# Splitting each weight piece of the down product in one instruction instead of two

## What is computed

```python
D_MODEL = 1024; SEQ = 512; DEC_BATCH = 8; DEC_SEQ = 8; D_FF = 4 * D_MODEL

def decoder_layer(x, shift0, s0, kv_past, logf_past, lw):
    ...
    x = x + mix @ lw['w_out']
    h2 = rms_norm(x, lw['mlp_norm'])
    x = x + jnp.square(jax.nn.relu(h2 @ lw['w_mlp_up'])) @ lw['w_mlp_down']
```

## Time and profile before

| | |
|---|---|
| median of 3 executions | 933.12 us (929.53 to 935.15) |
| the profiled execution, its own time | 931.69 us |
| its span, first to last instruction | 930.0 us |
| TensorE busy | 893.5 us (96%) |
| VectorE busy | 640.7 us (69%) |
| ScalarE busy | 451.7 us (49%) |
| mean granted TensorE clock, share of full speed | 0.996 |

### The profile page before, as it was taken

One profiled execution on the slowest core, in us unless ns is written; L12 is line 12 of the kernel. 1 busy time (PEld: TensorE's weight loads), 2 busy tenths in 40 slices (PEclk: granted clock), 3 DMA queues, 4 the chain that ended last, 5 costly groups with the idle time before them and its releaser, 6 DMA issues.

```text
span 930.0 us, 21268 instructions
## 1 busy us (share of the span) xinstructions
PE 893.5 (96%) x8588; PEld 768.9 (83%) x8588; DVE 640.7 (69%) x1083; ACT 451.7 (49%) x771; POOL 62.0 (7%) x95
## 2 busy tenths in 40 slices
PE   6999999999899999899999999999999999999998
PEld 5999899998887767666655789988998899889986
DVE  5563377647656773666564572789988988988796
ACT  6422536313241376685562543463575456535751
POOL 0000112114500000000000000100101000000000
PEclk9999999999999999999999999999999999999999
DMA  8542787762200677548897704896878722443343
GB/s 271 181 137 69 160 204 202 238 128 68 83 6 3 216 264 245 199 158 298 308 391 263 250 15 137 209 273 185 246 204 239 214 91 93 179 136 92 133 142 144
DMA packets 73163, 164.47 MB, mean 177 GB/s; under 512 B 5918, under 2 KB 32126, under 8 KB 70890
## 3 DMA queue, kind: packets, MB, share of 16 engines
q1 hardware_dynamic: 59370, 124.26, 38.9%
q0 software_dynamic: 13696, 38.85, 17.6%
HBM read 156.55 MB, written 40.10 MB: 211 GB/s over the span
## 4 chain that ended last, share of the span: by engine, by line
PE 81%; DVE 13%; ACT 2%; issue 2%; DMA 1%; DVEq 0%; ACTq 0%
PE PS L960 16%; PE PS L962 15%; PE PS L961 15%; PE PS L1152 7%; PE PS L1315 3%; PE PS L1387 2%; PE PS L1337 2%; PE PS L993 2%; DVE WL L2912 2%; PE PS L1301 2%; PE PS L1423 1%; PE PS L1275 1%; PE PS L1292 1%; PE PS L1627 1%; PE PS L1628 1%
## 5 line engine op out<-in xcount | busy, mean ns | idle before, releaser
L961 PE MATMUL PS<-WL,U 128*128 128x512 f32 x224 | 87.5, 391 | 0.0
L960 PE MATMUL PS<-WH,U 128*128 128x512 f32 x224 | 87.5, 390 | 0.0
L2025 ACT ACTIVATE WH<-Wraw 128x1024 fp32r<-128x1024 f32 x56 | 57.9, 1055 | 47.8 <-DMA Wraw<-tau 16.3
L2912 DVE TENSOR_TENSOR WL<-Wraw,WH 128x1024 fp32r<-128x1024 f32 x56 | 66.8, 1218 | 7.1 <-ACT WH L2025 7.1
L1152 PE MATMUL PS<-AR 64*64 64x64 f32 x1912 | 61.8, 219 | 4.6 <-issue 2.9
L1152 PEld LDWEIGHTS PS<-AR 64*64 64x64 f32 x1912 | 58.6, 135 | 8.1 <-issue 5.8
L960 PE MATMUL PS<-WR,HR 128*128 128x384 f32 (+1 forms) x184 | 63.7, 346 | 0.8 <-issue 0.8
L960 PE MATMUL PS<-h2H,WH 128*128 128x288 f32 x208 | 61.4, 295 | 0.5 <-DVE rc L3034 0.5
L961 PE MATMUL PS<-h2L,WH 128*128 128x288 f32 x208 | 61.2, 294 | 0.0
L962 PE MATMUL PS<-h2H,WL 128*128 128x288 f32 x208 | 61.2, 294 | 0.0
L1315 PE MATMUL PS<-cst,AR 128*128 128x128 f32 x384 | 53.5, 281 | 7.0 <-ACT W L1913 7.0
(11 more groups left out here) (436 smaller groups left out, 2309.2 us busy)
## 6 DMA issues: line engine op xcount, KB each, us to landing
AR<-in_cache_kv SPq DMA_DIRECT2D x120, 384.0 KB, 4.7
tau<-in_w_mlp_down POOLq DMA_DIRECT2D x24, 1024.0 KB, 9.1
Wraw<-tau SPq DMA_DIRECT2D x16, 1024.0 KB, 4.8
Wraw<-in_w_mlp_up SPq DMA_DIRECT2D x14, 1024.0 KB, 5.6
Wraw<-in_w_mlp_down SPq DMA_DIRECT2D x12, 1024.0 KB, 5.1
W<-in_w_in SPq DMA_DIRECT2D x6, 1536.0 KB, 8.9
QK<-in_cache_kv SPq DMA_DIRECT2D x8, 384.0 KB, 5.9
AR<-in_x_prompt SPq DMA_DIRECT2D x4, 512.0 KB, 7.0
```

Source lines behind the costliest of these rows:

```text
L960: mm(out, lH, rH, start=start, stop=False, skip_group_check=skip)
L961: mm(out, lH, rL, start=False, stop=False, skip_group_check=skip)
L2025: f(piece_half(WH, r, d, h), piece_half(Wraw, r, d, h), ACT.Copy).then_inc(w_hi, 1)
L2912: tt(piece_half(WL, r, d, h), piece_half(Wraw, r, d, h), piece_half(WH, r, d, h).bitcast(F32), SUB).then_inc(w_lo, 1)
```

## The change

Each piece of the down product is split by one ScalarE instruction and one VectorE instruction of 2048 columns, in place of two of each of 1024. `w_hi` and `w_lo` then grow by one a piece. TensorE's use of a piece is still counted by halves. The order of the instructions moves where the halves stood apart:

```diff
-        def split_at(r, d, h):
-            return 4 + 14 * r + 2 * d + h + 1
+        def split_at(r, d):
+            return 4 + 7 * r + d + 1
...
-        def half_free(r, d, h):
+        def piece_free(r, d):
 
             if d >= 2:
-                return dn_used, 14 * r + 2 * (d - 2) + h + 1
-            return pair_used(4 * r - 1, 2 * d + h) if r else (u_ps, 6 + 2 * d)
+                return dn_used, 14 * r + 2 * (d - 2) + 2
+            return pair_used(4 * r - 1, 2 * d + 1) if r else (u_ps, 6 + 2 * d)
...
-                    def split(h):
-
-                        pe.wait_ge(w_hi, split_at(r, d, h))
-                        pe.wait_ge(w_lo, split_at(r, d, h))
-
+                    pe.wait_ge(w_hi, split_at(r, d))
+                    pe.wait_ge(w_lo, split_at(r, d))
...
-            def half_hi(r, d, h):
+            def down_hi(r, d):
 
                 q = 11 * r + 4 + d
-                act.wait_ge(*half_free(r, d, h))
+                act.wait_ge(*piece_free(r, d))
                 act.wait_ge(in_raw[q % 2], 16 * (q // 2))
-                f(piece_half(WH, r, d, h), piece_half(Wraw, r, d, h), ACT.Copy).then_inc(w_hi, 1)
+                f(whole_piece(WH, r, d), whole_piece(Wraw, r, d), ACT.Copy).then_inc(w_hi, 1)
...
-                half_hi(r, 1, 0)
+                down_hi(r, 1)
                 relu_crossed(i)
                 square_quad(i, 1)
                 square_quad(i, 0)
-                half_hi(r, 1, 1)
                 mix_form_hi(r, 2)
                 down_splits(r)
...
-                half_lo(r, 2, 0)
-                half_done(r, 0)
+                piece_done(r, 0)
                 take_common(r, X_BANK, ADD if r else None)
-                half_lo(r, 2, 1)
+                down_lo(r, 2)
...
-                half_lo(r, 6, 0)
-                half_done(r, 4)
+                down_lo(r, 6)
+                piece_done(r, 4)
                 take_quarter(0, 1, Q5_BANK, ADD)
                 take_samples(1, S_BANKS[1], ADD)
-                half_lo(r, 6, 1)
...
                 crossed_sums(i)
-                half_lo(r, 1, 0)
+                down_lo(r, 1)
                 quad_low(i)
-                half_lo(r, 1, 1)
                 take_down(r)
```

More of the change, by code:

```diff
@@ L564, in piece_half, with whole_piece @@
             return ring[:, s, h * 1024:(h + 1) * 1024].rearrange("p (k c) -> p k c", k=2)
-        def half_free(r, d, h):
+        def whole_piece(ring, r, d):
+            return ring[:, (11 * r + 4 + d) % 2 if ring is Wraw else (d + r) % 2, :]
+        def piece_free(r, d):
             if d >= 2:
-                return dn_used, 14 * r + 2 * (d - 2) + h + 1
-            return pair_used(4 * r - 1, 2 * d + h) if r else (u_ps, 6 + 2 * d)
+                return dn_used, 14 * r + 2 * (d - 2) + 2
+            return pair_used(4 * r - 1, 2 * d + 1) if r else (u_ps, 6 + 2 * d)
         def pair_used(i, p):
@@ L2127, in down_splits @@
                         turned_hi(4)
-                    for h in range(2):
-                        half_hi(r, d, h)
+                    down_hi(r, d)
             def turned_hi(n):
@@ L2147, in _ @@
                 if n in (5, 7):
-                    for h in range(2):
-                        half_hi(0, n // 2 - 2, h)
+                    down_hi(0, n // 2 - 2)
                 if 4 <= n < 7:
@@ L2907, in sample_low, with down_lo @@
                 tt(HL[:, row, NS:2 * NS], us_raw[:, m % 2, :], HL[:, row, 0:NS].bitcast(F32), SUB).then_inc(u_lo, 1)
-            def half_lo(r, d, h):
-                dve.wait_ge(w_hi, split_at(r, d, h))
-                tt(piece_half(WL, r, d, h), piece_half(Wraw, r, d, h), piece_half(WH, r, d, h).bitcast(F32), SUB).then_inc(w_lo, 1)
+            def down_lo(r, d):
+                dve.wait_ge(w_hi, split_at(r, d))
+                tt(whole_piece(WL, r, d), whole_piece(Wraw, r, d), whole_piece(WH, r, d).bitcast(F32), SUB).then_inc(w_lo, 1)
             def mix_form_lo(r, d):
@@ L3061, in take_down @@
                 mix_sum(r, 4)
-                half_done(r, 1)
+                piece_done(r, 1)
                 take_quarter(1, 1, Q7_BANK, SUB)
-                half_lo(r, 3, 0)
-                half_lo(r, 3, 1)
+                down_lo(r, 3)
                 mix_form_lo(r, 4)
-                half_done(r, 2)
+                piece_done(r, 2)
                 take_quarter(0, 0, X_BANK, ADD)
                 take_samples(0, S_BANKS[0], ADD)
-                half_lo(r, 4, 0)
-                half_lo(r, 4, 1)
+                down_lo(r, 4)
                 mix_form_lo(r, 5)
-                half_done(r, 3)
+                piece_done(r, 3)
                 dve.wait_ge(y_ready, 10 * r + 3)
                 take_quarter(1, 1, Q5_BANK, ADD)
-                half_lo(r, 5, 0)
-                half_lo(r, 5, 1)
+                down_lo(r, 5)
                 mix_form_lo(r, 6)
@@ L3088, in take_down @@
                     form_lo(4 * r, 0)
[L3089 removed]
+                piece_done(r, 5)
                 take_common(r, X_BANK, SUB)
@@ L3112, in _ @@
                 if n in (5, 7):
-                    for h in range(2):
-                        half_lo(0, n // 2 - 2, h)
+                    down_lo(0, n // 2 - 2)
                 if 4 <= n < 7:
```

15 lines of the change are left out of this document (5 added, 10 removed).

## The result

Seven executions of each kernel on one chip: before 932.98 us in the median (929.53 to 935.71), after **942.19 us** (939.39 to 946.25). The ratio is 1.0091, with an interval of 1.0068 to 1.0115 (95%): 8.5 us slower. The prediction said 7.4 us more, 940.5 (936.5 to 944.0).

A forecast was written before the change was run, and what follows sets the result against it. The prediction took TensorE, busy 893.5 of 930.0 us, as the bound, so only later operands count. Its terms, 3.4 + 2.4 + 1.0 + 0.6 = 7.4 us, on the median of 933.12 gave 940.5 us, range 936.5 to 944.0.

The forecast's parts named there:

- The saving: All 28 pieces: wholes save 2.0 us of VectorE and 2.5 us of ScalarE time; worth nothing where TensorE does not wait.
- Round 0, 3.4 us: Lateness of TensorE at the end of round 0, from later whole splits: 3.4 us, ends 2.5 and 4.2.
- Piece 1: Round 0, piece 1: first product in steady flow at 616.7 in place of 614.30, TensorE 2.4 us late.
- The wait at `take_samples`: Round 0, at 623.43, where VectorE's chain sets the time: TensorE no longer idles 0.76 us; lateness there 1.6 us.
- piece 3: Round 0, piece 3: no slack, VectorE's whole starts 1.5 us later and TensorE's lateness becomes 2.5 us.
- Ends of rounds 1 and 2: Taking of piece 5 comes 3.0 us later against 2.0 us of slack: TensorE waits 1.2 us each, 2.4 us together.
- End of round 3: VectorE starts taking piece 5 at 921.23 in place of 920.21, and all that follows hangs on it: 1.0 us.
- Piece 2 in rounds 1 to 3: Piece 2's low split comes later: between 0 and 0.85 us each, taken as 0.2 each, 0.6 us together.
- What costs nothing: TensorE's fewer waits, and loads into `Wraw`, issued later by the same amounts as TensorE is: no cost.
- The third rival: Loads come late as well, adding 0.85 us once more in each of four rounds, 3.4 us: 943.9 us; chance 0.12.
- The first rival: TensorE's slack covers the later splits, leaving the saving alone, round 0 0.5 us shorter: 932.6 us; chance 0.05.
- the second: Rival: only round 0 pays, its 3.4 us, with the later rounds' ends in time: 936.5 us; chance 0.12.

The follow-up runs named there:

- piece 6 alone: The kernel before with only piece 6 split whole, in all four rounds, on ScalarE and VectorE; 938.91 us, ratio 1.0043.
- low split behind the takings: The changed kernel, all pieces whole, with piece 6's low split moved behind the takings of piece 4 instead of ahead of them; 938.69 us, ratio 1.0040.
- all but piece 6: The changed kernel with piece 6 in two halves again, in their old places; 936.89 us, ratio 1.0017.
- with the sums later: The changed kernel with GpSimd's weight sums for round 3 started only after piece 2 of round 1 is used; 940.45 us, ratio 1.0065.
- the copy by ScalarE: The kernel before, all in halves, with round 0's taking of piece 0 done by ScalarE instead of VectorE; 932.25 us, ratio 0.9961.

## Why the prediction was right, point by point

- **The saving** (2.0 us of VectorE, 2.5 of ScalarE, worth nothing): it is there, 1.6 and 3.7 us on the page, and worth nothing in time. For ScalarE the estimate took every piece as a pair of 1.99 us; halves that stood apart took 1.04 to 1.06 each. Without effect, since ScalarE waits for a slot, a load or VectorE anyway.
- **Round 0, 3.4 us**: 3.3. Piece 1: first product predicted at 616.7, which with the 5.0 us of this execution is 621.7; it is at 621.63, with 2.16 us of wait recorded. The wait at `take_samples` is gone and the lateness there 1.5 (1.6 predicted); piece 3 2.6 (2.5). The end came out at 0.7 more in place of 0.85.
- **Ends of rounds 1 and 2, 1.2 us each**: 1.3 and 1.2. At the end of round 2 the taking of piece 5 is 3.0 us later, as worked out, against a slack of 2.0 before. The experiment with piece 6 alone gives these waits by themselves, and the one with its low split behind the takings removes them. This step is shown, cause and size.
- **End of round 3, 1.0 us**: 1.2. The whole split of piece 6 starts 3.8 us after VectorE had nothing more to do, and the taking of piece 5 starts behind it and the takings of piece 4:

```profile
928.86 2.29 DVE L2907 TENSOR_TENSOR WL<-Wraw,WH 128x2048 fp32r<-128x2048 f32 x1 [3.83 <-ACT WH L2024]
...
933.63 0.69 DVE L3029 TENSOR_TENSOR us<-us,PS 128x512 f32<-128x512 f32 x1
```

  933.63 against 920.21 is 13.4, less 5.0: 8.4 us, the whole lateness, so nothing is gained or lost behind it.
- **Piece 2 in rounds 1 to 3, 0.2 us each**: this is the term that was mis-sized in the profiled execution. In rounds 2 and 3 it is 0.1 and 0.2. In round 1 it is **1.1**, above the 0.85 at which its range ended. The step that failed is the sentence under "What costs nothing": that the loads into `Wraw` are later by the same amounts as TensorE is. The load of this piece can only be issued when the slot is free, which is when the low split of piece 0 is done. It was issued 3.6 us later than before (707.33 less 698.76 less 5.0), where TensorE was 3.3 late, and lasted 9.7 us for 9.0, so it came 0.9 us later against TensorE. Before, ScalarE had already waited 3.2 us for it, but that row was not among those read:

```profile
ACT WH L2025 <- DMA Wraw<-in_w_mlp_down: 7.0, 4, 3.2
```

  The whole had used up the 1.8 us of slack that hid such a load. Where the load came soon, whole on both engines, the place cost 0.1 us (all but piece 6, and with the sums later), so there the term was near enough.
- **The third rival** (loads late in every round, 3.4 us) is not what happened: ScalarE's waits for `Wraw` fell from 16.3 + 7.0 us to 5.3 + 7.7, because ScalarE and TensorE are later themselves. But its mechanism is at work in one place of this execution, where a load runs beside GpSimd's sums.
- **The first rival** is excluded by TensorE's waits, 7.5 us in six places, **the second** by those at the starts of rounds 2 and 3 (755.59 and 847.23).

The sum was 7.4 and the stretch showed 8.4; 0.9 of the difference is the one term. With the sums moved the same sum measures 7.4 in the trace. How many of the seven timed executions had the late load is not known, so the medians (8.5 us, 6.3 to 10.7 by the interval) bear out the sum and not its last microsecond. In the Trainium skill (Perfetto Trace Analysis, section Optimizing Scalar/DVE Operations) the last sentence of the passage is that breaking up instructions may allow work to be completed sooner where Scalar and Vector are not saturated but cause bubbles elsewhere. The traces agree, and set it against the same section's advice on grouping: 0.06 us of VectorE's busy time saved a piece, and 7.5 us of TensorE's waits in place of 1.3.

## What to carry to other kernels

Where two engines work on a piece one behind the other and a third waits for both, an instruction's length is also the latency of the hand-over: price a merge by when its first consumer can start, against the slack at that place, and only then by the overhead that it saves. Merge where the piece has slack (here rounds 1 to 3, and behind the takings), keep halves where a slot has just come free and others queue behind the split. And where the first engine already waits for a load, the slack of the last one is what hides it: once a merge has used that slack up (here 1.8 us), whatever puts the load off, or slows it, is paid in full.

## What the runs showed of the hardware that was not expected

**The clock fell after some of the waits and not after others.** In the kernel with all wholes but piece 6, TensorE waits 2.17 us for piece 1 of round 0, and 0.8 us later its matmuls run at half pace for 3.4 us:

```profile
622.54 0.47 PE L970 MATMUL PS<-WH,U 128*128 128x512 f32 x1 [2.17 <-DVE WL L2932]
...
623.32 0.63 PE L970 MATMUL PS<-WH,U 128*128 128x512 f32 x1
623.75 0.63 PE L971 MATMUL PS<-WL,U 128*128 128x512 f32 x1
```

They start 0.43 us apart in place of 0.23: the 1.2 GHz level. By stretches of 5 us, first this kernel, then after, each from just before the first product behind the same wait (columns as in the earlier trace rows):

```profile
622.00:627.00 5.00, 4.46 (x13) 3.57 (x14) 5.00 (x6) 0.82 (x1) 0.00 (x0) 0.66 1.09 221
```

```profile
621.00:626.00 5.00, 4.37 (x19) 3.65 (x20) 5.00 (x6) 0.91 (x1) 0.00 (x0) 1.00 1.06 205
```

The waits are alike (2.17 and 2.16 us), the clock is 0.66 in the one and 1.00 in the other, and 13 matmuls against 19 were done. Such a stretch costs TensorE some 1.6 us (lateness 4.0 behind it, 2.4 in after). Here 0.4 us of that was left at the end of round 0: at the next waits VectorE's chain took most of it in, but later VectorE waits for TensorE (1.14 us at 644.49, 0.76 in after) and passes the rest on. Behind the wait of 2.2 us at round 1's piece 2 (low split behind the takings) it came on top with 1.7 us, behind that of 2.1 us at the start of round 1 (the copy by ScalarE) with 1.5 us. The profiles of all kernels hold seven waits of 2.1 to 2.4 us, of which five were followed by such a stretch and two not (after, and the change with the sums later); behind no shorter wait, 1.5 us at the longest, did the clock fall. What decides was not tried; an execution with a wait of over 2 us may pay it or not, so one profile can't give the size of such a wait's cost.

**The stretch ahead of the change varied more than the change is worth.** At the `WR` instruction, with identical work up to there, the eleven other profiled executions stood between 1.7 us earlier and 6.2 us later than that of before. Without this correction the profiles would read 3.0 us for piece 6 alone, 9.5 for all the others and 13.4 for the whole change.

**A load of 1 MB into `Wraw` beside GpSimd's sums in DRAM took 5 us in one execution and 11 in another.** The load of round 1's piece 2 took 9.0 us before, 9.7 after and 11.0 with the low split behind the takings, but 5.3 to 7.9 us in the seven other kernels that run sums at that time; with the sums moved away it took 4.9 and 5.0. What decides between them was not tried. The median of all such loads on the page of after is 5.5 us:

```profile
Wraw<-in_w_mlp_down SPq DMA_DIRECT2D x12, 1024.0 KB, 5.5
```
